# A 2,048-wide two-layer trunk kernel: the Strassen stage's weight sums as adding transfers, its input sums on VectorE, another order of its seven products

## The reference

```python
def conv_mixer(h, w_in, conv_w, w_out):
    u, b_gate, c_gate, z = jnp.split(h @ w_in, 4, axis=-1)
    y = b_gate * causal_depthwise_conv(c_gate * u, conv_w)
    return (y * jax.nn.silu(z)) @ w_out
...
        h = rms_norm(x, norm_pre[layer])
        if layer % 2 == 0:
            y = ab_mixer(h, ...)
        else:
            y = conv_mixer(h, c_w_in[o], c_conv[o], c_w_out[o])
        x = x + rms_norm(y, norm_post[layer])
```

## Time and profile before

| | us |
|---|---|
| median of 3 runs | 2413.51 |
| lowest and highest | 2410.75, 2414.1 |
| the profiled execution's own time | 2409.57 |
| its span | 2407.8 |
| TensorE busy in the span | 2327.4 |
| VectorE, ScalarE, GpSimd busy | 1635.4, 931.8, 610.4 |

### The profile page before, as it was taken

How to read it: one execution, slowest core, us unless ns; L and a number is a source line. 1 busy time by engine, 2 the same in 40 slices (tenths; PEclk the granted TensorE clock), 3 DMA queues, 4 the chain that set the end, 5 groups by cost and what they waited for, 6 DMA issues and landing times.

```text
span 2407.8 us, 34136 instructions
## 1 busy us (share of the span) xinstructions
PE 2327.4 (97%) x13689; PEld 2013.7 (84%) x13689; DVE 1635.4 (68%) x1904; ACT 931.8 (39%) x1553; POOL 610.4 (25%) x315
## 2 busy tenths in 40 slices
PE   8999999999999999999999989999999999999998
PEld 6888888888787788888787769999999999788776
DVE  6676766755556577632756889899999998523755
ACT  5333333324344455422434533333333333322434
POOL 4000010101011010011303465655665564111400
PEclk9999999999999999999999889999999999999999
DMA  5222223223322234522222413233322223423222
GB/s 199 96 77 78 83 69 91 71 91 100 102 90 71 90 102 156 201 92 92 79 79 80 148 53 122 91 113 114 113 84 94 106 106 111 170 97 123 70 70 88
DMA packets 84873, 244.56 MB, mean 102 GB/s; under 512 B 16992, under 2 KB 20224, under 8 KB 84736
## 3 DMA queue, kind: packets, MB, share of 16 engines
q1 hardware_dynamic: 84256, 241.06, 29.6%
q10 hardware_dynamic: 480, 1.59, 0.2%
HBM read 231.59 MB, written 11.03 MB: 101 GB/s over the span
## 4 chain that ended last, share of the span: by engine, by line
PE 79%; DVE 11%; POOL 4%; issue 3%; ACT 2%; DMA 0%; DVEq 0%; ACTq 0%; POOLq 0%; SPq 0%
PE acc L1125 16%; PE acc L1127 16%; PE acc L1126 16%; DVE weights_lo L2339 5%; PE m L1621 2%; PE m L1624 2%; PE m L1623 2%; PE acc L1483 2%; PE acc L1621 2%; PE acc L1484 2%; PE acc L1624 2%; PE acc L1623 2%; PE acc L1488 2%; DVE weights_lo L1651 1%; PE m L1299 1%
## 5 line engine op out<-in xcount | busy, mean ns | idle before, releaser
L1125 PE MATMUL acc<-input_hi,weights_hi 128*128 128x512 f32 (+1 forms) x1880 | 745.2, 396 | 17.8 <-DVE weights_lo L1651 17.2
L1127 PE MATMUL acc<-input_hi,weights_lo 128*128 128x512 f32 (+1 forms) x1880 | 722.0, 384 | 0.0
L1126 PE MATMUL acc<-input_lo,weights_hi 128*128 128x512 f32 (+1 forms) x1880 | 720.9, 383 | 0.0
L1651 DVE TENSOR_TENSOR weights_lo<-weights_raw,weights_hi 128x1024 fp32r<-128x1024 f32 x288 | 398.1, 1394 | 180.4 <-ACT weights_hi L605 179.8
L1125 PEld LDWEIGHTS acc<-input_hi,weights_hi 128*128 128x128 f32 x1880 | 355.3, 189 | 98.3 <-DVE weights_lo L1651 18.5
L1127 PEld LDWEIGHTS acc<-input_hi,weights_lo 128*128 128x128 f32 x1880 | 354.5, 189 | 71.7
L1126 PEld LDWEIGHTS acc<-input_lo,weights_hi 128*128 128x128 f32 x1880 | 355.6, 189 | 64.7 <-issue 1.9
L605 ACT ACTIVATE weights_hi<-weights_raw 128x1024 fp32r<-128x1024 f32 x288 | 298.9, 1057 | 185.7 <-PE acc L1127 152.9
L2487 POOL TENSOR_TENSOR small<-small 128x4 f32<-128x4 f32 (+1 forms) x19 | 25.4, 1336 | 848.2 <-DVE small L1890 371.5
L1621 PE MATMUL m<-input_hi,weights_hi 128*128 128x256 f32 x672 | 192.6, 287 | 18.9 <-DVE work L2396 10.1
L1623 PE MATMUL m<-input_lo,weights_hi 128*128 128x256 f32 x672 | 191.3, 285 | 0.0
(11 more groups left out here) (376 smaller groups left out, 4416.0 us busy)
## 6 DMA issues: line engine op xcount, KB each, us to landing
weights_raw<-in_ab_w_in SPq DMA_DIRECT2D x126, 512.0 KB, 3.7
weights_raw<-in_c_w_in SPq DMA_DIRECT2D x72, 512.0 KB, 4.6
weights_raw<-in_m_w_kv SPq DMA_DIRECT2D x32, 512.0 KB, 3.8
weights_raw<-in_ab_w_out SPq DMA_DIRECT2D x32, 512.0 KB, 4.3
weights_raw<-in_m_w_q SPq DMA_DIRECT2D x32, 512.0 KB, 3.7
weights_raw<-in_c_w_out SPq DMA_DIRECT2D x32, 512.0 KB, 4.3
work<-in_c_w_in SPq DMA_DIRECT2D x28, 512.0 KB, 5.1
weights_a<-in_c_w_in SPq DMA_DIRECT2D x28, 512.0 KB, 3.8
```

The lines of the kernel that those rows point to most:

```text
L1125: pe.matmul(out, w_hi[:, o:o + P], hi(kt), start=kt == first_kt, stop=False)
L1126: pe.matmul(out, w_hi[:, o:o + P], lo(kt), start=False, stop=False)
L1127: last = pe.matmul(out, w_lo[:, o:o + P], hi(kt), start=False, stop=kt == last_kt)
L1651: TTO(w_lo[:, s * CW:(s + 1) * CW], raw[:, c * CW:(c + 1) * CW], w_hi[:, s * CW:(s + 1) * CW].bitcast(F32), ALU.subtract).then_inc(lo_read ...
```

## The change

Nothing of what is computed changes, but the signs and the place of the sums do.

- **Weight sums.** GpSimd computes none. It issues four transfers per pair that add their source into SBUF (`accum_op=ALU.add`): A22 from DRAM into the buffer of A21 (S1), A11 from DRAM into a second copy of A21 (S3), then S1's buffer into that of A11 (S2), and S2's into that of A12 (S4). With additions alone S1, S2 and S3 are A21 + A22, A11 + A21 + A22 and A11 + A21; S4 is A12 + S2. The signs go into the input sums and into VectorE's additions. SP issues a fifth load per pair (A21 again, for S3). The buffer r1 of A12 and S4 is double now, that of A22 single. GpSimd's ring for transfers is larger (`dynamic_dma_scratch_size` 128 to 1024).
- **Input sums.** VectorE computes the 32 of them in place, ahead of its own low parts; ScalarE rounds them in another order.
- **Order of the products.** From A11, S1, S2, A12, S3, S4, A22 to A11, S3, A12, S1, S2, S4, A22. ScalarE copies one more product out of PSUM (product 1, to a new buffer `seventh`); VectorE's additions of a pair stay five in number.
- **Rows of norms.** The two products with them per group move from GpSimd to VectorE (`br`, `zr`).
- **Around the stage.** The residual is saved in two halves, after the loads of chunks 9 and 11; the kept part of the result comes back to `Y` rather than `X`, and the residual's reload no longer waits for the split of the result.

The core of the diff:

```diff
-S_ORDER = ("A11", "S1", "S2", "A12", "S3", "S4", "A22")
-S_BANK, S_FRESH = (0, 2, 1, 0, 1, 2, 1), 3
+S_ORDER = ("A11", "S3", "A12", "S1", "S2", "S4", "A22")
+S_BANK, S_FRESH = (0, 1, 0, 2, 1, 2, 1), (0, 1, 3, 5)
...
-TURNED_AT = {11: (0, 1), 12: (2,), 13: (3, 4), 14: (5, 6), 15: (7,)}
+TURNED_AT = {10: (0,), 11: (1, 2), 12: (3,), 13: (4, 5), 14: (6,), 15: (7,)}
...
             def s_loads(q):
...
                 if q < 2:
+                    sp.wait_ge(lo_ready, C_C + 15 + q)
                 else:
-                    sp.wait_ge(s_lo, 7 * (q - 2) + 3)
-                    sp.wait_ge(s_sum, sums(q - 2, "S4"))
+                    sp.wait_ge(s_lo, 7 * (q - 2) + 4)
+                    sp.wait_ge(s_sum["S2"], 16 * (q - 1))
+                s_load(q, 2, s_raw["r2"][q % 2], s_in["r2", q % 2])
...
+                    sp.wait_ge(s_lo, 7 * (q - 2) + 5)
+                    sp.wait_ge(s_sum["S4"], 16 * (q - 1))
+                s_load(q, 0, s_raw["r0"][q % 2], s_in["r0", q % 2])
...
+                    sp.wait_ge(s_lo, 7 * (q - 2) + 6)
+                s_load(q, 1, s_raw["r1"][q % 2], s_in["r1", q % 2])
+                if q > 1:
+                    sp.wait_ge(s_lo, 7 * (q - 1) + 2)
+                if q:
+                    s_load(q, 2, s_s3(q), s3_in)
+                    sp.wait_ge(s_lo, 7 * q)
+                s_load(q, 3, s_raw["r3"][0], a22_in)
...
+            def wino_sums(q):
+                block = 4 * (8 * (0, 2, 1, 3)[q % 4] + q // 4 + 1)
+                quarter = lambda at_: dram["c_w_in"][P * (block + at_):P * (block + at_ + 1), :]
+                r0, r1, r2 = (s_raw[r][q % 2] for r in ("r0", "r1", "r2"))
+                pool.wait_ge(s_in["r2", q % 2], 16 * (q // 2 + 1))
+                pool.dma_start(r2, quarter(3), accum_op=ALU.add).then_inc(s_sum["S1"], 16)
+                pool.wait_ge(s3_in, 16 * (q + 1))
+                pool.dma_start(s_s3(q), quarter(0), accum_op=ALU.add).then_inc(s_sum["S3"], 16)
+                pool.wait_ge(s_lo, 7 * q + 1)
+                pool.wait_ge(s_sum["S1"], 16 * (q + 1))
+                pool.dma_start(r0, r2, accum_op=ALU.add).then_inc(s_sum["S2"], 16)
+                pool.wait_ge(s_lo, 7 * q + 3)
+                pool.wait_ge(s_sum["S2"], 16 * (q + 1))
+                pool.dma_start(r1, r0, accum_op=ALU.add).then_inc(s_sum["S4"], 16)
...
+            def turned_sums(kt):
+                low, high = ([xt(k)[:, h * HT:(h + 1) * HT] for h in range(2)] for k in (kt, kt + 8))
+                dve.wait_ge(turn_scaled, 2 * kt + 2)
+                TTO(before_third(kt), high[1], low[1], ALU.subtract).then_inc(turn_in, 1)
+                TTO(before_first(kt), low[0], low[1], ALU.subtract).then_inc(turn_in, 1)
...
+                    if s % 7 == 2:
+                        act.wait_ge(s_used, i)
+                        if q:
+                            act.wait_ge(s_ev, evacs(q - 1, "base"))
+                        act.activation(v7, s_bank(q, 1), ACT.Copy).then_inc(s_p7, 1)
```

More of the change, by code:

```diff
@@ L973, in s_split @@
                 q, name = i // 7, S_ORDER[i % 7]
-                if name in ("A11", "A12", "A22"):
-                    r, n = ("r1", 0) if name == "A12" else (home[name], q % 2)
-                    act.wait_ge(s_in[r, n], 16 * ((q if r == "r1" else q // 2) + 1))
+                if name == "A22":
+                    act.wait_ge(a22_in, 16 * (q + 1))
+                elif name in ("A11", "A12"):
+                    act.wait_ge(s_in[home[name], q % 2], 16 * (q // 2 + 1))
                 else:
-                    act.wait_ge(s_sum, sums(q, name))
+                    act.wait_ge(s_sum[name], 16 * (q + 1))
                 if i < S_SLOTS:
@@ L2374, in conv_first @@
                     for kt in TURNED_AT.get(c, ()):
-                        for n in range(3):
-                            turned_low(kt, n)
+                        turned_sums(kt)
+                        if kt:
+                            turned_low(kt - 1)
+                turned_low(7)
                 for i in range(S_SLOTS):
@@ L2430, in conv_step @@
                             op0=ALU.mult, op1=ALU.add).then_inc(*WV.did("conv"))
[L2431 to L2432 removed]
+                elif step == 21:
+                    dve.wait_ge(s_ev, evacs(q + 2, "C21"))
+                    dve.wait_ge(s_c11, q + 3)
+                    TTO(head2(bb), head2(bb), both_rows(rs[:, :]), ALU.mult).then_inc(*WV.did("br"))
+                elif step == 22:
                     dve.wait_ge(*WV.last())
@@ L2617, in _ @@
                 if r == 1:
-                    turned_sums()
-                    wino()
+                    for q in range(S_PAIRS):
+                        wino_sums(q)
             for t in range(TT):
```

254 lines of the change are left out of this document (109 added, 145 removed).

## The result

| | before | changed |
|---|---|---|
| median, us | 2414.1 | 2425.07 |
| lowest and highest, us | 2410.75, 2415.4 | 2423.97, 2427.39 |
| the profiled execution's own time, its span | 2409.57, 2407.8 | 2427.39, 2425.6 |

The changed kernel is slower by 0.48%: the ratio is 1.0048, with a 95% interval of 1.0033 to 1.0063. The forecast was 2373.

A forecast was written before the change was run, and what follows sets the result against it. VectorE, slowed by GpSimd's arithmetic, was taken to hold TensorE in the stage. Stage 36.2 plus start 3.8 gave 40.0 us: 2409.57 becomes 2369.6, plus 3.9 for the median, forecast 2373; range 2358 to 2440, likeliest 2358 to 2385.

The forecast's parts named there:

- what bound the kernel before: In the 609.7 us stage, GpSimd's arithmetic slows VectorE, whose late additions hold TensorE; the change was to win 36.2 us there.
- VectorE's new list: VectorE's work per group of four pairs in the stage, without GpSimd's arithmetic: 54.6 of 80.64 us, no longer the bound.
- The rival of splits that stay long: In the stage, GpSimd's descriptor writing slows VectorE's splits as its arithmetic did: 2400 to 2415 us; chance 0.06.
- A start of GpSimd's made late by VectorE's operations with a constant: In the stage, port locking delays a transfer's start 1 us in one pair of four, at most 7 us; not summed.
- the start: Ahead of the stage's first product, VectorE does the input sums: first product at 1434.2 instead of 1438.0, 3.8 us won.
- The end: After the stage, TensorE's 3.89 us stall at the output projection's chunk 2 stays even: nothing counted, 4 us either way.
- the step on L: L, from wait's end to landing of S2's or S4's transfer, taken as 6.3 us; the two in series allow 7.6.
- S2's own bound of 12.4: In a pair, S2's transfer may take up to 12.4 us from A11's split before S2's own split is late.
- The third term: In the pair's loop, after S4 lands: splits of S4, A22 and the next A11, about 5 us.
- rival 2: In the stage, S2's and S4's serial transfers become the bound, slower than before: 2447 at L = 9, 2515 at 10.2; chance 0.22.
- rival 1: In the stage, adding transfers take part of the gain, L 7.6 to 8.3 or S2 queued: 2378 to 2408 us; chance 0.12.
- the mark of full engines: In the stage, if groups exceed 84 us, a DMA share over 0.9 means the engines, below it the latency.

The follow-up runs named there:

- The unhindered versions with and without the change: Without: kernel before, GpSimd's sums on 32 columns, 2373.25 us. With: changed kernel, S2's transfer at 128 columns, 2367.74, or loads of A11, A12, A22 at 128, 2366.5.
- the version with the loads ahead: Changed kernel with SyncE's loads of the next pair's A21, A11 and A12 put before this pair's load of A22, all bytes kept: 2380.75 us.

## Why the prediction was wrong

The forecast was 40 us faster; the kernel came out 11 us slower. That 2425 lies inside the stated 2358 to 2440 is no merit of the forecast: the part of the range above 2385 was held for the rivals.

**Right: what bound the kernel before.** GpSimd's arithmetic held the stage. With the sums on 32 columns the stage loses 39.1 us, for the forecast's 36.2; that the whole comes to 2373.25, the forecast's own number, is chance, since the start and the order of products are the old ones there. In the changed kernel each group of splits in the stage has a mean of 1.22 us where the earlier trace rows had 3.30 beside GpSimd.

**Right: VectorE's new list.** 54.6 of 80.64 us were worked out. Where the changed kernel runs unhindered (S2's transfer small) it is 53.1, from 263.5 busy us in the 400 between 1500 and 1900. The rival of splits that stay long found nothing here. A start of GpSimd's made late by VectorE's operations with a constant, weighed at up to 7 us, is not needed to account for the loss; no run tests it.

**Right enough: the start.** The gap ahead of the first product went from 7.36 to 1.60 us, the first product came at 1435.7 and not at 1434.2 (between 1435.2 and 1437.8 in the eight kernels of this study that share this start). VectorE's wait at chunk 12, worked out as 1.6 us, is 1.43, and the three after it are 0.4 each where 1 was taken; what was not worked out is that TensorE stands 3.08 us for that chunk. The unhindered versions with and without the change differ by 5.5 to 6.8 us (2373.25 against 2367.74 and 2366.5), for start, order and end together; 3.8 was in the sum. **The end** stayed even, with a stall of 4.01 for 3.89:

```profile
2081.83 0.50 PE L1135 MATMUL acc<-input_hi,weights_hi 128*128 128x512 f32 x1 [4.01 <-DVE weights_lo L1664]
```

**Wrong: the step on L.** The forecast rested on one inequality, -3.3 + 2L <= 11.9, with L = 6.3 for both transfers. The prediction had seen the burst ("S2 may come 3 us late, inside its margin"), but it set these 3 us against S2's own bound of 12.4 and not into the sum of the two transfers in series. With them, by its own terms, a pair comes to 5 + 9.3 + 6.3 = 20.6, over 20.16 already. The measured terms, from the two pairs shown:

| term of the loop | forecast | measured |
|---|---|---|
| S2's issue to S4's issue | 6.3 | 11.0 (11.71 and 10.26) |
| S4's issue to its split | 6.3 | 4.9 |
| from there to the next S2's issue | 5 | 6.6 (the rest of 22.55) |
| a pair | 17.6, so TensorE's 20.16 | 22.5 |

Of the 6.3, the adding transfer without the company of loads was 5.3, and it measures 4.8 to 4.9; the company was 1 for both, and it measures 4.8 at S2 and nothing at S4. The third term was short because it held the splits only. VectorE's list has its additions and, in this pair, a gating operation of 1.22 us between them (1725.76 in the timeline shown), and ran them one after the other once the low part of S4 came late. So what happened is the mild form of rival 2, decided where it was said to be decided, at a pair of 21.8: 22.5 is 0.7 over it, 28 times, 20 us, less what the start gave. Its price per transfer was wrong (not two slow ones, one slow and one quick). Two slips in its sums change nothing: rival 1's 2378 counts from 2373 and its 2408 from 2369.6 (from 2373 it is 2412), and 1.06 + 1.21 + 0.2 is 2.47, not 2.45.

**The two prices of an adding transfer.** In engine time it is 2.8 us (49.5% of 500 us for 46.18 MB in pieces of 0.524 MB), near the upper end of the 1.5 to 3.0 that was taken; a load is 1.5. The factor of 1.8 agrees nearly with the Trainium skill's "Collectives: The Full Stack" (The bandwidth ceiling), by which two source reads halve the rate; the estimate of 5.3 for its time alone is near the 4.8 to 4.9 of the rows. The price that decided was the other one: what was issued ahead of it. On that, the Trainium skill's "DMA: Bandwidth & Descriptors" (Queues, rings and completion order) says that an engine takes its queues in turn, a packet from each. By this alone, if such a packet is no more than one load's part on an engine, S2 would be through before the last load of the burst, and to make that load small would change nothing; it took 2.1 us off S2 (9.6 to 7.5), and S2 of 64 KB still took 5.7. Here the measurement decides: no packet of S2 moved in the first 5 us after its issue at 1705.41; from 1710.4 on, with 144 packets of its queue and 215 of SyncE's in 6 us, the two queues do move side by side.

**What it would have taken to see it.** The DMA share of 0.86 in the stage lay below the 0.9 that the prediction set as the mark of full engines, and it pointed to the latency, as said. The question left out was which transfers are issued in the 2 us before the one on the path. It could have been answered before the run, from the waits in SyncE's and GpSimd's lists: low part 7q for the burst, 7q + 1 for S2.

## What to carry to other kernels

A transfer that takes the place of an engine's instruction costs little work but gets a place among the other transfers, and here its time was set by what was issued just ahead of it: cost it with that company, and put that figure into every bound in which the transfer stands, above all where two of them are in series. Where engine A slows engine B, moving A's work to B itself can be cheaper than moving it to a third: here one sum cost 1.23 us on VectorE and 9.6 as a transfer on the path. Before a load is delayed to make room, look at what waits in order behind it.

## What the runs showed of the hardware

- An adding transfer of 512 KB from SBUF to SBUF lands in 4.8 to 4.9 us when no burst of whole loads is under way at its issue, some 1 us over a plain load of that size (3.8 in the earlier trace rows), though it holds the engines for 2.8 us instead of 1.5. What is issued behind it does it little harm: S4's took 4.9 us with the adding transfers of S1 and S3 issued 0.55 and 1.10 us after it, and 4.8 with these made small.
- Its time behind a burst grew by about the time the burst needed, 1.6 us for each load of 512 KB. An adding transfer of 64 KB behind the burst took 5.7 us, more than one of 512 KB without it. Of the growth, 2.2 us lie before its first packet (3.6 us after issue for 1.5, medians).
- A DMA share of 0.92 over 100 us went with a TensorE that never stood (1800 to 1900 in the version with the loads ahead), and one of 0.66 with a TensorE that stood 7% of the time (S1's and S3's transfers small): the share told nothing of the end.
- VectorE kept 1.22 to 1.23 us for a sum or split of 128x1024 with GpSimd issuing transfers beside it, at up to 83 busy us in 100, where it took up to 3.30 us beside GpSimd's addition.
